# The ring of weight halves in a Strassen-like feed-forward: u2 is split a block ahead, and three kinds of weights change ring places

## What is computed

```
def swiglu(h, wg, wu, wd):
    return (jax.nn.silu(h @ wg) * (h @ wu)) @ wd
xp = xp + 0.5 * swiglu(rmsnorm(xp, norm_ffn1[i]), w_ffn1_gate[i], w_ffn1_up[i], w_ffn1_down[i])
```

## Time and profile before

| what | value |
|---|---|
| median of 3 runs | 2475.04 us |
| lowest and highest | 2470.79 and 2477.73 us |
| the profiled execution | 2488.74 us |
| its span, first to last instruction | 2486.9 us |
| mean granted TensorE clock | 0.98 |
| TensorE busy | 2338.0 us, 94% |
| VectorE, ScalarE, GpSimd busy | 1676.6, 1172.1 and 480.2 us |

### The profile page before, as it was taken

How to read it: one execution, slowest core, us unless ns; L and a number is a source line. 1 busy time by engine, 2 the same in 40 slices (tenths; PEclk the granted TensorE clock), 3 DMA queues, 4 the chain that set the end, 5 groups by cost and what they waited for, 6 DMA issues and landing times.

```text
span 2486.9 us, 47320 instructions
## 1 busy us (share of the span) xinstructions
PE 2338.0 (94%) x17889; PEld 2250.6 (91%) x17889; DVE 1676.6 (67%) x2599; ACT 1172.1 (47%) x2162; POOL 480.2 (19%) x342
## 2 busy tenths in 40 slices
PE   7899999999999999999799999899999999899998
PEld 7899899875999999999799999889999999799998
DVE  7778775546555555547877777877776666877774
ACT  4445454464455555534445454445453224454542
POOL 0243430000000000000244330234340000244340
PEclk9899999979999999999999999899999999899999
DMA  4778764310211111203678764678763333577772
GB/s 129 169 190 202 182 165 122 88 44 25 60 30 49 49 45 43 61 18 94 161 196 199 185 166 113 152 180 200 186 175 102 94 90 98 131 184 195 186 201 81
DMA packets 502368, 313.30 MB, mean 126 GB/s; under 512 B 36352, under 2 KB 484950, under 8 KB 502152
## 3 DMA queue, kind: packets, MB, share of 16 engines
q1 hardware_dynamic: 486420, 253.67, 35.8%
q0 software_dynamic: 15552, 56.63, 13.1%
q10 hardware_dynamic: 180, 0.11, 0.0%
HBM read 250.89 MB, written 2.87 MB: 102 GB/s over the span
## 4 chain that ended last, share of the span: by engine, by line
PE 57%; DMA 15%; DVE 12%; issue 6%; ACT 5%; POOL 4%; SPq 1%; ACTq 0%; DVEq 0%; POOLq 0%
PE ps L2030 15%; PE ps L552 6%; PE ps L556 6%; PE ps L554 6%; PE ps L951 5%; PE ps L953 5%; PE ps L952 5%; DMA wsum75b<-raw 5%; DMA raw<-in_w_ffn_up 5%; DMA raw<-in_w_ffn_down 3%; POOL wsum L737 2%; POOL wsum L735 1%; DVE w_lo L653 1%; DVE w_lo L683 1%; DMA wsum<-raw 1%
## 5 line engine op out<-in xcount | busy, mean ns | idle before, releaser
L951 PE MATMUL ps<-hs,w_hi 128*128 128x260 f32 x1440 | 416.4, 289 | 43.1 <-DVE w_lo L653 17.8
L952 PE MATMUL ps<-hs,w_hi 128*128 128x260 f32 x1440 | 411.8, 286 | 0.0
L953 PE MATMUL ps<-hs,w_lo 128*128 128x260 f32 x1440 | 411.4, 286 | 0.0
L951 PEld LDWEIGHTS ps<-hs,w_hi 128*128 128x128 f32 x1440 | 276.0, 192 | 51.7 <-DVE w_lo L653 21.7
L952 PEld LDWEIGHTS ps<-hs,w_hi 128*128 128x128 f32 x1440 | 276.8, 192 | 0.0
L953 PEld LDWEIGHTS ps<-hs,w_lo 128*128 128x128 f32 x1440 | 275.9, 192 | 0.0
L2077 ACT ACTIVATE ksq<-ps 128x384 f32<-128x384 f32 (+1 forms) x384 | 146.7, 455 | 196.6 <-PE ps L2030 196.6
L951 PE MATMUL ps<-hs,x_hi 128*128 128x260 f32 x688 | 200.8, 292 | 27.8 <-DVE x_lo L653 15.3
L737 POOL TENSOR_TENSOR wsum<-wsum,raw 128x512 f32<-128x512 f32 x108 | 210.9, 1953 | 8.5
L952 PE MATMUL ps<-hs,x_hi 128*128 128x260 f32 x688 | 197.9, 288 | 0.0
L953 PE MATMUL ps<-hs,x_lo 128*128 128x260 f32 x688 | 197.7, 287 | 0.0
(11 more groups left out here) (409 smaller groups left out, 6341.5 us busy)
## 6 DMA issues: line engine op xcount, KB each, us to landing
raw<-in_w_ffn_gate SPq DMA_DIRECT2D x88, 512.0 KB, 4.0
raw<-in_w_ffn_up SPq DMA_DIRECT2D x88, 512.0 KB, 5.2
raw<-in_w_ffn_down SPq DMA_DIRECT2D x64, 512.0 KB, 5.5
wsum<-raw POOLq DMA_DIRECT2D x56, 512.0 KB, 5.6
wsum75b<-raw POOLq DMA_DIRECT2D x52, 512.0 KB, 5.8
cache<-in_cache_latent SPq DMA_DIRECT2D x128, 128.0 KB, 2.0
raw<-in_w_ffn_down SPq DMA_DIRECT2D x32, 384.0 KB, 3.5
raw<-in_w_conv_in SPq DMA_DIRECT2D x24, 512.0 KB, 3.8
```

The lines of the kernel that those rows point to most:

```text
L951: nc.tensor.matmul(o, hi[:, kc], mh[:, xc], start=start and k == 0, stop=False, skip_group_check=goes_on)
L952: nc.tensor.matmul(o, hi[:, kc], ml[:, xc], start=False, stop=False, skip_group_check=goes_on)
L953: mm = nc.tensor.matmul(o, lo[:, kc], mh[:, xc], start=False, stop=k == KH - 1, skip_group_check=goes_on)
```

## The change

The ring places and the order of work change together. M4 is now split before M63, in the block ahead, right behind the finishing adds, and takes the place of the M75 of the block ahead. M63 takes the place that M4 of the block ahead leaves, and M75 that of the block's own M12. TensorE keeps its order. `part_lo_made` now counts M12, M4, M63, M75; `part_used` counts in TensorE's order as before.

```diff
-        M12, M63, M75, M4 = 0, 2, 4, 6
+        M12, M4, M63, M75 = 0, 2, 4, 6
+        PLACE = {M12: 0, M63: 2, M4: 4, M75: 6}
@@ slot_free
+                if self.kind in "SD":
+                    if q == M75:
+                        act.wait_ge(part_used, self.end(0, 2))
+                    elif q == M4 and self.b == 3:
+                        act.wait_ge(unit_used, self.u0 + 2)
+                    else:
+                        act.wait_ge(part_used, self.p - {M12: 4, M4: 2, M63: 0}[q])
+                    return
@@ raw_free
-                sp.wait_ge(part_lo_made, who.done if j else who.end(M12, 2))
+                sp.wait_ge(part_lo_made, who.end(M4, 2) if j else who.end(M12, 2))
@@ ring
-            s = (4 + bk.local + q - q % 2) % RING
+            y = q - q % 2
+            s = (4 + bk.local + (PLACE[y] if bk.kind in "SD" else y)) % RING
@@ ffn_pe, block
-                pe.wait_ge(part_lo_made, bk.done)
@@ ffn_act, block
+                keep_first(bk)
                 m75_hi(act, bk)
-                keep_first(bk)
-                m4_hi(act, bk)
                 keep_second(bk)
...
                 keep_third(bk)
                 if not nxt.plain:
-                    m63_hi(act, nxt)
+                    m4_hi(act, nxt)
                 if bk.gated:
                     silu(bk)
+                if not nxt.plain:
+                    m63_hi(act, nxt)
@@ ffn_dve, block
+                second_made(bk)
                 m75_lo(dve, bk)
-                second_made(bk)
                 if not early:
-                    m4_lo(dve, bk)
...
                     if done and not done.last:
                         pair_mix(dve, done)
-                    m4_lo(dve, bk)
                     first_begun(bk)
-                    if done:
-                        last_lo(dve, done) if done.last else pair_lo(dve, done)
+                    if done and done.last:
+                        last_lo(dve, done)
                     plain_lo(dve, nxt) if nxt.plain else first_lo(dve, nxt)
                 first_made(bk)
                 up_made(bk)
+                if not nxt.plain:
+                    m4_lo(dve, nxt)
                 if bk.out:
                     first_out(bk)
                 if not nxt.plain:
                     m63_lo(dve, nxt)
+                if early and done and not done.last:
+                    pair_lo(dve, done)
```

More of the change, by code:

```diff
@@ L494, in slot_free @@
                     act.wait_ge(unit_used, self.u0 + 1)
-                elif self.b == 3 and q == M75:
-                    act.wait_ge(unit_used, self.u0 + 2)
                 else:
@@ L692, in m4_lo @@
         def m4_lo(dve, bk):
-            dve.wait_ge(part_hi_made, bk.done)
+            dve.wait_ge(part_hi_made, bk.end(M4, 2))
             nc.vector.tensor_tensor(ring(LO, bk, M4), bk.raw_half(1, 1), ring(HI, bk, M4), ALU.subtract).then_inc(part_lo_made, 2)
@@ L1020, in keep_second @@
             def keep_second(bk):
-                act.wait_ge(part_used, bk.end(M63))
+                act.wait_ge(part_used, bk.p + 3)
                 nc.scalar.copy(gate_t[:, 0:HALF], ps[:, bk.bank, 0:HALF]).then_inc(kept, 1)
             def keep_third(bk):
-                act.wait_ge(part_used, bk.end(M75))
+                act.wait_ge(part_used, bk.p + 5)
                 nc.scalar.copy(bk.third(), ps[:, bk.bank, 0:HALF]).then_inc(kept, 1)
@@ L1055, in ffn_act @@
             set_hi(act, at, 2)
+            set_hi(act, at, 3)
             silu(own[2])
-            set_hi(act, at, 3)
+            m4_hi(act, own[3])
             m63_hi(act, own[3])
@@ L1114, in first_begun @@
             def first_begun(bk):
-                dve.wait_ge(part_used, bk.end(M63, 2))
+                dve.wait_ge(part_used, bk.p + 4)
                 dve.wait_ge(kept, 3 * bk.s + 2)
@@ L1119, in first_made @@
             def first_made(bk):
-                dve.wait_ge(part_used, bk.end(M75, 2))
+                dve.wait_ge(part_used, bk.p + 6)
                 dve.wait_ge(added, ADDS * bk.idx + C1_D)
@@ L1211, in ffn_dve @@
             up_lo(dve, own[2])
+            plain_hid(own[1])
             scaled_dve(dve, at, 2)
             set_mix(dve, at, 2)
-            plain_hid(own[1])
-            scale_gate(own[2])
+            first_lo(dve, own[3])
+            set_lo(dve, at, 2)
             scaled_dve(dve, at, 3)
             set_mix(dve, at, 3)
-            first_lo(dve, own[3])
-            set_lo(dve, at, 2)
+            scale_gate(own[2])
             set_lo(dve, at, 3)
+            m4_lo(dve, own[3])
             m63_lo(dve, own[3])
```

## The result

| what | before | changed kernel |
|---|---|---|
| median | 2476.39 us (4 runs) | 2579.51 us (4 runs) |
| lowest and highest | 2470.79 and 2487.82 | 2572.73 and 2597.76 |
| ratio with 95% interval | | 1.0408 [1.0372, 1.0444] |
| span of the profiled execution | 2486.9 | 2595.9 |

The change makes the kernel slower by 103 us. That is inside the range of the prediction and 31 us above its number. The profiled executions, 2597.8 and 2488.7 us, lie 18 and 12 us above these medians, so the traces lie 109.0 us apart.

A forecast was written before the change was run, and what follows sets the result against it. TensorE, 94% busy, was taken as the bound, with about 80 us of waits to be had. Terms of 62, 8 and 4 us made 74, so 2475 became 2549 us; own range 2523 to 2580, with rivals 2505 to 2590.

The forecast's parts named there:

- The stall of M4: Pair block: mixing behind M75's split delays pair_hi, first_hi and keep_third, so M4 begins 1.6 us late.
- pair and follower: Pair block with the block after it: 2.2 us more each, 28 times, 62 us (48 to 81).
- The start of the follower: M12's split at the follower's start: 0.4 us later if the split is fast, 1.05 if it meets GpSimd.
- The stall of M75 in the follower: Follower: pair_lo behind M63's split makes M75's split 1.3 us late in both cases.
- 28 count: Of 32 pair blocks, all but the first fast block of each feed-forward pay 2.2 us: 62 us.
- Matmuls, transfers and their sizes stay; no cost: Whole kernel: work of TensorE and the transfers is unchanged, so nothing was added for it.
- Down and last blocks: Chain of the sums gets second_made ahead of M75: 39 waits before M63, 0.2 us each, 8 us (0 to 16).
- The start of a feed-forward: plain_hid and scale_gate change places with operand sets, four times: 4 us (0 to 8).
- Rival 1: The chain of the sums binds the S blocks as well, giving 2580 us; chance 0.17.
- rival 3: Nothing changes: the stalls that go (M12's 41.9 us) match those that come, 2475 us; chance 0.04.
- Rival 4: Faster, 2422 us, with 34 us of M12 gone, if the mixing slips by less than 0.57 us; chance 0.08.

The follow-up runs named there:

- Experiment 3: Changed kernel, with keep_third ahead of pair_hi on ScalarE in the 28 pair blocks: 2529.77 us, ratio 1.0200 to the kernel before.
- Experiment 2: Changed kernel, with pair_lo back ahead of M12's split in all 28 pair blocks: 2531.10 us, ratio 1.0224 to the kernel before.
- Experiment 1: Changed kernel, with pair_lo back ahead of M12's split only where a down block comes next (8 blocks): 2554.01 us, ratio 1.0295.
- experiment 6: Kernel before, with M12's split ahead of pair_lo in 24 pair blocks, not where a down block follows: 2461.05 us, ratio 0.9932.
- experiments 7: Kernel before, with SyncE's copies for the sums held until M4, not M75, of two blocks ahead is split: 2484.28 us, ratio 1.0018.
- 9: Kernel of experiment 6, with keep_first ahead of M75's copy only in blocks without mixing: 2468.92 us, ratio 0.9957.
- 10: Kernel 9, with SyncE's copies for the sums also held until M4's split, in blocks without mixing: 2486.39 us, ratio 1.0031.
- Experiment 4: Changed kernel, with VectorE's and ScalarE's preparing blocks of each feed-forward in the order of before: 2580.40 us, ratio 1.0396.

## Why the prediction was right, and where it was not

**The stall of M4, term "pair and follower".** Right in place, cause and size. The mixing behind M75's split, `pair_hi`, `first_hi` and `keep_third` one behind the other: worked out as 1.6 us late, measured 1.5 in the undisturbed pair blocks, which take 11.7 us. Experiment 3 takes the row away by moving `keep_third` alone.

**The start of the follower.** The forecast took a value between two ends; it was the fast one. In S6 M12's split takes 1.23 us, and S7 begins without a gap. Over all it is nearer to fast too:

```profile
L661 DVE TENSOR_TENSOR w_lo<-raw,w_hi x72: 1212/1366/2350, 82.7 to 2535.3; 128x1024 fp32r<-128x1024 f32 x72
```

The median is 1366 ns where the earlier trace rows has 2022. The split's place had moved in relation to GpSimd's sums, and with it its duration (in S6 the second sum ends at 267.14, and the split begins at 267.32); the row of before was carried over to another place.

**The stall of M75 in the follower.** Right: 1.3 forecast, 1.35 in S7, followers 11.5 us where the clock held. Experiment 2 shows the cause. S6 and S7 together take 23.2, 1.8 over the 21.4 of before, near the fast end of 1.7, and 2.2 was taken. What the forecast left out is that M75's split can meet GpSimd's sums too. It took 1.22 us in 12 of the 20 followers that are S blocks, with waits of 1.30 to 1.36 in 11 of them and none in one. In the other 8 a sum had begun before it; it took 1.63 to 2.35, and TensorE waited 1.8 to 2.7 us.

**The step that failed: "28 count".** `pair_lo` was charged with 2.2 us in each of 28 pairs, as if the follower were always an S block. In 8 of the 28 it is the first down block, which reads the very set that `pair_lo` makes, before its first matmul. In the kernel before, `pair_lo` stood ahead of M12's split, and that wait was short (10 us for all eight). Now TensorE waits 45.3 us there, the matmuls of these blocks take 17 us longer at the lower clock, and some 7 us of later waits have gone: 45.6 us more in all. The forecast had charged these eight blocks with 1.3 us each of the 2.2, about 10 us. Experiment 1 shows the place, and gives 25 us as its worth.

**The clock, a term that was missing.** "Matmuls, transfers and their sizes stay; no cost" is true of the work and not of its time: TensorE was busy 33.5 us longer. Of the gaps of 2.2 to 3 us between matmuls of the fast blocks, 9 of 10 were followed by matmuls at 1.2 GHz; of those above 3 us, all 16; of those of 1 to 1.6 us, 10 of 42. The changed kernel has 26 gaps above 2.2 us, the kernel before 4. So pair blocks with their followers, 23.2 us where the clock held, took up to 27.4 in the two middle feed-forwards, in part by the clock and in part by the longer waits ahead of M75. In all twelve traces together 80 of 83 gaps above 3 us were followed by matmuls at 1.2 GHz, and 43 of 63 gaps of 2.2 to 3 us. Experiment 3 agrees: with the stall of M4 gone it has 407 slow matmuls and not 558. No run held the gaps and changed the clock, so its share is worked out from rows and not isolated.

**Down and last blocks.** +8 was forecast; between the two traces the 24 other down blocks gained 12.4 and the last ones 3.8. The argument priced the 0.35 us of `second_made`, and took each transfer in the chain as it was in the earlier trace rows. The chain answers now like this (timeline of GpSimd, while D4 and D5 run):

```profile
311.61 0.87 POOL L739 DMA_DIRECT2D wsum<-raw  x1 [10.73 <-DMA raw<-in_w_ffn_down]
...
316.28 1.28 POOL L743 TENSOR_TENSOR wsum<-wsum,raw 128x512 f32<-128x512 f32 x1 [3.80 <-DMA wsum<-raw]
317.64 2.17 POOL L745 TENSOR_TENSOR wsum<-wsum,raw 128x512 f32<-128x512 f32 x1
```

From the start of the accumulating transfer (311.61) to the first sum it takes 4.67 us; in the earlier trace rows it runs from 307.26, and the second sum begins at 314.68, which here comes 6.03 us after the start and there 7.42. On average over the 24 other down blocks the chain from M75's split to the sums fell from 18.7 to 15.8 us, 1.3 of it in this transfer, 0.5 each in the way to the row's issue, the row's landing and the sums. That the parts became shorter is measured. That the new ring did it is not shown: the gaps ahead of M63 in these blocks fell from 17.0 to 5.7 us, but the trace of the kernel before stands alone with its 17.0, and kernels 6, 7 and 9, which keep the old ring, have 5.4, 5.4 and 9.1. So a part of this gain may belong to that one execution. Why the parts became shorter is open as well: the raw rows are now asked for at other times, and experiments 7 and 10 show that the transfer shortens when the copies start later, but in neither did the time follow.

**The start of a feed-forward.** Sized at 4 us, at most 8; the four first fast blocks took 12.0 more. The wait for the sets grew by 22, and the 10 us of wait ahead of the first matmul went. It was costed as three operations of 0.69 that change places. What moved besides is the scaling and mixing of the fourth operand set (3.0 us), from ahead of `set_lo` of the third set to behind it, with `scale_gate` (0.69) and 1.16 of waiting for ScalarE's copy after it. The two `set_lo`, one piece of 4.01 us before, now lie 4.8 us apart (62.49 to 64.54, and 69.33 to 71.38 in the first feed-forward), and TensorE waits 6.2 us for the second. Experiment 4 shows that this order makes the wait; in the time of the whole kernel it can tell nothing of it.

**The sum, and the luck in it.** Against the 109 us between the traces the forecast's terms stand like this: pair blocks and S followers 61 for 52 forecast, first down blocks 46 for 10, other down and last blocks, with the S blocks behind the first down group, -17 for +8, start 12 for 4, and outside the fast blocks 7 for 0. That the time lies inside the range is in part luck: the first down blocks cost 36 us more than their term, and 25 of these were given back by blocks that were forecast to lose and gained. The measured median of 2579.5 is at the very end of what the mechanism gave by itself, 2523 to 2580.

**The rivals.** Rival 1 named nearly the measured time (2580) for a reason that did not hold: the chain of the sums takes 15.6 us in the S blocks between the two groups of down blocks, less than before (16.3), and the gaps ahead of M63 halved. Of M12's 41.9 us, which the forecast and rival 3 took as stalls that repeat in the loop, 9.7 lay at the starts of the feed-forwards. Rival 4's condition, the mixing less than 0.57 late, is far from met. Of the 34 us of M12 that it counted on, experiment 6 removes 22 by exchanging two instructions, but in the followers most of it comes back ahead of M63.

## What to carry to other kernels

When an instruction is moved later, look for every reader of what it makes, in each kind of block it occurs in, and price the most pressing one: the loop's usual follower may not be the one that waits. When the order on a full engine is changed, ask what stands behind the moved piece on the same engine; here two pieces, one in front of a PSUM copy and one in front of a split, cost about 50 us each. Moving a piece out of one packet's way does not remove it: `pair_lo` held up whichever split came next, and its exchange with M12's split on the old order gained 17 us in all, little of that in the followers it was made for. And a long stall of TensorE costs more than itself: behind 25 of the 26 gaps above 2.2 us of the changed kernel the matmuls ran at half the clock. Last, when a wait's row shrinks, add up the gaps at that place before calling it won: here rows were renamed, and at the start of a feed-forward a wait moved from ahead of a packet into it.

## What the hardware showed

**Vector and GpSimd instructions that meet.** VectorE at the end of S7, and GpSimd's sums there:

```profile
274.93 1.22 DVE L691 TENSOR_TENSOR w_lo<-wsum,w_hi 128x1024 fp32r<-128x1024 f32 x1
...
276.40 2.00 DVE L661 TENSOR_TENSOR w_lo<-raw,w_hi 128x1024 fp32r<-128x1024 f32 x1
...
275.19 2.13 POOL L743 TENSOR_TENSOR wsum<-wsum75b,raw 128x512 f32<-128x512 f32 x1 [4.62 <-DMA wsum75b<-raw]
277.40 2.15 POOL L745 TENSOR_TENSOR wsum<-wsum,raw 128x512 f32<-128x512 f32 x1
```

Alone, the VectorE splits take 1.22 us and the GpSimd sums 1.28. The first sum starts while the split of M75 runs (to 276.15) and ends at 277.32, 1.17 after that; M12's split ends at 278.40, 1.08 after the first sum; the second sum ends at 279.55, 1.15 after the split. So they take turns, and each pays what is left of the one ahead, not always a whole instruction. This is what the Trainium skill says in "SBUF — State Buffer", section "SBUF: two separate sides": an exclusive lock, held for a whole instruction. The prediction read from it that a meeting always costs the slow figure; the rows between the two levels, as this one of 2.00, correct that. Who comes first decides who pays: of the 20 splits of M75 in the S followers, the 8 that began after a sum had begun took 1.63 to 2.35 us, and the 12 others 1.22, while 11 of these had a sum begin beside them, which ended 1.16 to 1.18 us after the split.

**Spread.** Runs of the changed kernel lie 25 us apart and those of experiment 4 31 us, four runs each, against 12 us over seven runs in experiment 6. The mean granted clock goes from .961 to .969 over the changed kernel's runs, with the slowest run at the lowest. That long gaps make the spread is not shown: experiments 1 and 3, with 18 and 15 gaps above 2.2 us, spread over 9 us in four runs, and the kernel before, with 4 such gaps, over 22 us in 28 runs.
